# One decoder layer, prompt and samples: window copies spread over the projection, the second sample's chunks loaded early, the samples' sums a step earlier

## The chip, the cores and the metric

One NeuronCore of a Trainium2 chip runs the whole kernel in one launch. The metric is device time in microseconds (us). TensorE (PE) multiplies; VectorE (DVE), ScalarE (ACT) and GpSimd (POOL) compute elementwise; SyncE (SP) computes nothing and issues most of the DMAs; ACT issues the others. All arithmetic is float32; products that need the precision are made from a high part rounded to fp32r and the low remainder.

## The reference

One layer (D_MODEL 1024) for 512 prompt tokens and for 8 samples of one token each, the samples with 2048 cached positions in 16 pages of 128. Cut to what matters:

```python
z = rmsnorm(x) @ w_in                      # 1024 -> 2840 columns
q_sb, k_sb, v_sb, q_n, kv_c, kv_s, kv_w, gates = split(z)
# stick-breaking heads
s = q_sb @ k_sb.T / 8
log_1m = where(mask, log_sigmoid(-s), 0)
after = cumsum(log_1m, reverse=True) - log_1m
o_sb = where(mask, exp(log_sigmoid(s) + after), 0) @ v_sb
# NSA heads: compressed keys of chunks of 16, chosen blocks of 64, a window of 512
kc, vc = mlp(chunks of cached kv_c)        # silu(x @ w1) @ w2 on 32 positions
o_n = g0 * attend(kc, vc) + g1 * attend(top 16 blocks) + g2 * attend(window)
x = x + concat(rmsnorm(o_sb), rmsnorm(o_n)) @ w_out
x = x + square(relu(rmsnorm(x) @ w_up)) @ w_down
y = rmsnorm(x)
```

The new keys and values are outputs too, among them each sample's window buffer shifted by one row (`win_s`, 511 old rows of 1 KB copied).

## The kernel before

The engines run their own programs and meet through counting semaphores; the order on each engine is the order written in its program. The stages that the change touches follow each other:

**Projection.** `w_in` is worked through in 10 blocks of 284 columns (`NCB`, `CB`). Two buffers `win[u]` take the raw blocks; ACT rounds them (`win_high`, line 1261), DVE takes the remainder (`win_low`, line 1671), and PE makes 24 matmuls (8 slices of depth, 3 products) for each of four token tiles (`z_rows`). Between tiles 1 and 2 of block n stand 16 narrow matmuls for the 8 samples with the raw block n+1 (`z_samples`), so PE waits there for the load of block n+1. SP issues that load when DVE's one-element `memset` (line 1697) says that tile 3 of block n-1 is done. In the first block (`begin`) the remainder of slices 0 to 3 is made by POOL (line 2258), that of slices 4 to 7 by DVE (line 1660), and DVE also makes the low part of the activations (`gained_low`, line 1637). Ahead of the loop over the blocks ACT waits for the constants and issues the eight window copies (line 1284), HBM to HBM, 511 KB each.

**Samples' keys.** For each of 8 samples SP loads in `load_keys` 16 chunk DMAs of 128 KB for the *next* sample's compression (`load_chunks`, line 499, into `nat`, two homes in turn), 16 pages of selection keys (line 542, buffers `kquad`), 16 pages of stick-breaking keys (line 545, buffers `kring`) and the window (line 548). POOL reorders chunks (`permute`), PE transposes and multiplies (`compress`) and between the parts transposes the keys (`keys_T`), DVE scores the stick-breaking keys. Chunks of sample 0 come during the projection. `nat[1]` first serves the prompt's own compression (`nat_in10`), so sample 1's chunks are loaded only in `load_keys(0, 0, True)`.

**Attention.** 48 steps, written out for each engine: 16 of stick breaking, then 32 of NSA. The samples' small steps stand between them: `sample_sums` on PE at step 3 (8 wide float32 matmuls), `sample_logs` on DVE, an exponential on ACT at step 4, the accumulator's `memset` at step 4. The samples' values are spread by `value_steps` over the steps: page pairs (8 matmuls of 128x256 each) from step 5 on, 3, 3, 2 a sample for the first four samples, then one or two a step.

Of the kernel before, what the change touches and what calls it, by code (L numbers as in the profile page):

```python
# [21 lines left out]
ds = bass.ds  # L22

P = 128
# [3 lines left out]
B = 8  # L28
# [32 lines left out]
def value_steps():  # L61

    pairs, quads = [()] * (STEPS + 2), [()] * (STEPS + 2)
    at = 5
    for b in range(B):
        m = 0
        for n in ((3, 3, 2) if b < 4 else (2, 1, 1, 1, 1, 1, 1)):
            pairs[at] = tuple((b, m + j) for j in range(n))
            m, at = m + n, at + 1
    at = SB_U + 1  # L70
    for b in range(B):
        q = 0
# [44 lines left out]
def shape_constants():  # L117
# [3 lines left out]
    def put(name, a):  # L121
# [41 lines left out]
    "start_act": ["rt"] * 5 + ["w_hi_first", "gates_e"],  # L163
    "samples_pe": ["c_sc", "g_mm", "m_T", "c_scT", "m_b", "c_pT", "s_c", "c_imp", "c_selT", "c_mask", "m_den", "m_T", "m_b", "m_den", "v_ss"],
    "samples_dve": ["s_abs", "m_max", "c_s", "c_kbd", "m_diag", "s_sp", "c_nm", "m_sub", "s_suf", "c_p", "m_sum", "c_pg", "s_d", "acc_set", "c_sel",
                    "c_selx", "c_selm", "m_max", "m_rec", "m_diag", "m_sub", "m_sum", "m_rec", "w_set", "v_sq", "v_st", "v_cols"],
# [52 lines left out]
def decoder_step(nc, A, O):  # L219
    with ExitStack() as ctx:  # L220
# [115 lines left out]
        xT = [view(hT_at + i * 2048, KD, KVH, P) for i in range(2)]  # L336
        nat_at[1] = r.take(4096)
        nat = [[view(nat_at[u] + 2048 * half, CH // 2, 2, KVH, DH) for half in range(2)] for u in range(2)]
        hid = [view(r.take(256), KVH, P) for _ in range(4)]
        qb = view(r.take(2 * 512), 2, 512)  # L340
        kqT = view(x_at + 4228, 4, P)

# [127 lines left out]
        def _(sp):  # L470
# [39 lines left out]
            for u in range(2):  # L510
                load_block(u, FIRST // 2, u * CB)
                load_chunks(page_ids(8 * u), 0, u)
            load_columns(FIRST // 2 + 1, (NCB - FIRST) // 2 - 1, 2 * CB)

            sp.wait_ge(sem("rope_done"), T5)
# [3 lines left out]
            for t in range(T5):  # L519
                sp.wait_ge(sem(f"z_ev{t}"), NCB + 1)  # L520
            sp.wait_ge(sem("cmp_stored"), 16)
            sp.dma_start(nat[1][0][0:2 * (NCP + 1)].rearrange("p t k h d -> p (t k h d)"),
                O["cmp_p"][0, 0].rearrange("(c t) k h d -> c (t k h d)", t=CH // 2)).then_inc(sem("nat_in10"), 16)
            sp.dma_start(O["sb_p"][0, 0].rearrange("(t p) k h d -> p t (k h d)", p=P), z[:, 0:NT, O_KS:O_KS + 1024]).then_inc(sem("sb_stored"), 16)
# [29 lines left out]

            with sp.Fori(0, 3) as i:
                for u in range(2):
                    load_keys(i, u, True)
# [101 lines left out]
        def _(pe):  # L659
# [34 lines left out]
            def z_rows(i, u, t, begin=False):  # L694

                pe.wait_ge(sem(f"z_ev{t}"), i * 2 + u + 1)
                for k in range(KD):
                    if begin:
                        pe.wait_ge(sem("hT_ev"), k + 1)
                        if k == 0:  # L700
                            pe.wait_ge(sem("z_zero"), 2)
                        if k == KD // 2:
                            pe.wait_ge(sem("w_lo0"), 1 + 1)
                    for n, (h_, w_) in enumerate(((hT_r, win_hi_r), (hT_r, win_r), (hT_lo1_r, win_hi_r))):
                        ins = mm(bank[t][:, 0:CB], h_[:, k, t * P:(t + 1) * P], w_[u][:, k, :], k == 0 and n == 0, k == KD - 1 and n == 2)
                ins.then_inc(sem("z_mm"), 1)
# [414 lines left out]
            for s in range(STEPS + 2):  # L1121
# [16 lines left out]
                if 1 <= s < SB_U + 1:  # L1138
                    sb_sum(s - 1)
                if s == 3:  # L1140
                    sample_sums()
# [87 lines left out]
        def _(act):  # L1229
# [52 lines left out]
            wb, wo = A["state_nsa_win_kv"][0], O["win_s"][0]  # L1282
            for b in range(B):
                act.dma_start(wo[b, 0:WIN - 1].rearrange("(o s) k h d -> o (s k h d)", o=1),  # L1284
                    wb[b, 1:WIN].rearrange("(o s) k h d -> o (s k h d)", o=1)).then_inc(sem("kv_out"), 16)
            for turn, turns, col in COLUMNS:
                more = turn + turns < NCB // 2
                with act.Fori(0, turns if more else turns - 1) as i:
                    win_high(1, i + turn)
                    z_out(0, i, turn, col)  # L1290
                    win_high(0, i + turn + 1)
                    z_out(1, i, turn, col)
                if not more:
# [197 lines left out]
            for s in range(STEPS + 2):  # L1491
                if s in (5, 7, 9, 11):
                    cp_exp((s - 5) // 2)
                if s < SB_U:
                    sb_ln(s)
                if s == 4:
                    act.wait_ge(*signal("s_d", 1))
# [120 lines left out]
        def _(dve):  # L1618
# [35 lines left out]
            for t in range(2, NT):  # L1654
                row_scale(t, t + 2)
            for k in range(KD):
                gained_low(k)
                if k == 2:
                    dve.wait_ge(sem("w_hi0"), 1)
                    V.tensor_tensor(win_r[0][:, KD // 2:], win[0][:, KD // 2:], win_hi[0][:, KD // 2:], ALU.subtract).then_inc(sem("w_lo0"), 1)  # L1660
            dve.wait_ge(sem("z_zero"), 1)
# [309 lines left out]
            def small_steps(s):  # L1971
# [11 lines left out]
                if s == 3:  # L1983
                    cmp_groups()
                if s == 4:
                    dve.wait_ge(*signal("s_d", 1))
                    V.memset(bank[7][:, :], 0.0).then_inc(sem("samples_dve"), 1)
                    rank_greater()
                if s in (5, 7, 9, 11):
# [15 lines left out]
            def small_steps_late(s):  # L2005
# [3 lines left out]
                if s == 1:  # L2009
                    later_pages()  # L2010
                if s == 3:
                    sample_logs()
# [239 lines left out]
        def _(pool):  # L2252
# [4 lines left out]
            pool.wait_ge(*signal("w_hi_first", 1))  # L2257
            G_.tensor_tensor(win_r[0][:, 0:KD // 2], win[0][:, 0:KD // 2], win_hi[0][:, 0:KD // 2], ALU.subtract).then_inc(sem("z_zero"), 1)  # L2258

            pool.wait_ge(sem("qkT_mm"), 15)  # L2260

            def permute(c, kv, half, n):

                for hh in range(KVH):
                    ins = G_.tensor_copy(per(kv, hh, half)[0:n], nat[c % 2][half][0:n, :, kv, hh, :])
                ins.then_inc(sem("perm"), 1)

            pool.wait_ge(sem("nat_in10"), 16)
            for kv in range(2):
                permute(1, kv, 0, 2 * (NCP + 1))  # L2270
            for c in range(B):
                for kv in range(2):
                    for half in range(2):
                        if kv == 0:
                            pool.wait_ge(sem(f"nat_in{c % 2}{half}"), (c // 2 + 1) * 128 + (16 if c % 2 and half == 0 else 0))
                        if c == 0 and half == 1:
# [3 lines left out]
                        elif c:  # L2280
                            pool.wait_ge(sem("xT_mm1"), 4 * (c - 1) + 2 * kv + 2)
                        permute(c, kv, half, P)
            for n in range(1, KD):
# [38 lines left out]
```

## Time and profile before

| | |
|---|---|
| median of 3 runs | 1145.65 us (1145.42 to 1149.24) |
| the profiled execution | 1144.81 us, its span 1143.0 us |
| PE busy | 1061.2 us (93%) |
| DVE, ACT, POOL busy | 619.5, 391.3, 63.3 us |
| DMA | 177.59 MB, mean 155 GB/s |
| chain of waits, by engine | PE 61%, SP's queue 18%, issue 7%, DVE 5%, DMA 5%, ACT 3% |

The first row is what is compared; the second is the execution from which all durations come. The chain of waits follows the work that ended last back to what released it, so its shares say which engine set the end. An engine's busy share is an average over stages with different limits.

### The profile page before, as it was taken

What the parts mean: (1) busy time and instruction counts of PE and PEld (TensorE: products, weight loads), DVE (VectorE), ACT (ScalarE), POOL (GpSimd) and SP (SyncE); (2) the same over time, 40 slices, a digit from 0 to 9 for tenths busy, and PEclk for the clock granted to TensorE, in tenths of its full rate; (3) what the DMA queues carried; (4) which work ended last, traced back from release to release, by engine and by line L of the source; (5) the groups of instructions that cost most, each with busy time, mean ns of one, the idle gap of its engine ahead of it and who ended that gap; (6) DMA issues with size and microseconds to landing.
All of it is one profiled execution on the core that took longest, in us unless ns stands there. A gap on an engine that the chain in (4) does not pass through costs nothing.

```text
span 1143.0 us, 22964 instructions
## 1 busy us (share of the span) xinstructions
PE 1061.2 (93%) x8284; PEld 933.5 (82%) x8284; DVE 619.5 (54%) x1056; ACT 391.3 (34%) x729; POOL 63.3 (6%) x83
## 2 busy tenths in 40 slices
PE   6899998988989998899999889999999999998995
PEld 5899997887878886555555558999999999998995
DVE  5334664777768776775455445445533335553334
ACT  4111122333333335656454354322221112222124
POOL 1000003111111100000000000100000000000000
PEclk8899996989989895999998999999999999999998
DMA  8427539999999853356666762223333332333221
GB/s 295 151 89 201 129 98 227 250 248 258 269 261 260 246 182 120 121 175 226 204 208 194 214 203 75 75 74 92 110 92 91 92 83 84 91 92 93 90 78 75
DMA packets 180323, 177.59 MB, mean 155 GB/s; under 512 B 13128, under 2 KB 140869, under 8 KB 177893
## 3 DMA queue, kind: packets, MB, share of 16 engines
q1 hardware_dynamic: 178536, 169.72, 52.5%
q10 hardware_dynamic: 1724, 7.04, 1.8%
q8 instruction: 39, 0.64, 0.2%
q14 instruction: 24, 0.19, 0.1%
HBM read 170.83 MB, written 10.06 MB: 158 GB/s over the span
## 4 chain that ended last, share of the span: by engine, by line
PE 61%; SPq 18%; issue 7%; DVE 5%; DMA 5%; ACT 3%; ACTq 1%; POOL 0%; DVEq 0%; POOLq 0%
PE bank L664 59%; SPq L578 4%; SPq L499 3%; SPq L542 3%; SPq L545 3%; PE bank L668 3%; SPq L492 2%; DMA high_arena<-in_w_in_dram 2%; SPq L566 2%; DMA low_arena<-in_cache_nsa_slc_kv_dram 1%; DMA low_arena<-in_consts_dram 1%; DMA high_arena<-out_cmp_p_dram 1%; ACTq L1284 1%; DVE high_arena L2231 0%; DMA high_arena<-in_cache_nsa_slc_kv_dram 0%
## 5 line engine op out<-in xcount | busy, mean ns | idle before, releaser
L664 PE MATMUL bank<-high_arena 128*128 128x254 f32 (+8 forms) x1864 | 242.0, 349 | 11.9 <-ACT high_arena L1321 6.1
L664 PEld LDWEIGHTS bank<-high_arena 128*128 128x128 f32 (+5 forms) x1864 | 186.9, 153 | 49.8 <-issue 9.2
L2163 DVE TENSOR_TENSOR w_low<-high_arena,w_high 128x1024 fp32r<-128x1024 f32 x72 | 90.1, 1252 | 81.0 <-ACT w_high L1484 71.0
L1484 ACT ACTIVATE w_high<-high_arena 128x1024 fp32r<-128x1024 f32 x72 | 76.4, 1061 | 144.7 <-PE bank L664 144.7
L668 PE MATMUL bank<-low_arena 128*128 128x128 f32 (+3 forms) x658 | 103.2, 298 | 16.4 <-DMA low_arena<-in_cache_nsa_slc_kv_dram 10.4
L664 PE MATMUL bank<-a_high,w_high 128*128 128x256 f32 (+1 forms) x512 | 103.7, 284 | 5.3 <-issue 2.9
L668 PEld LDWEIGHTS bank<-low_arena 128*128 128x128 f32 (+3 forms) x658 | 83.0, 157 | 28.9 <-issue 12.3
L664 PE MATMUL bank<-h_high,w_high 128*128 128x256 f32 (+1 forms) x512 | 103.0, 282 | 1.8 <-DVE h_low L2187 1.8
L664 PE MATMUL bank<-a_low,w_high 128*128 128x256 f32 (+1 forms) x512 | 103.2, 283 | 0.0
L664 PE MATMUL bank<-h_low,w_high 128*128 128x256 f32 (+1 forms) x512 | 103.2, 283 | 0.0
L664 PE MATMUL bank<-h_high,w_low 128*128 128x256 f32 (+1 forms) x512 | 103.1, 283 | 0.0
L664 PE MATMUL bank<-a_high,w_low 128*128 128x256 f32 (+1 forms) x512 | 102.9, 282 | 0.0
L664 PE MATMUL bank<-w_in_high,h_high 128*128 128x284 f32 x320 | 97.3, 304 | 2.7 <-POOL w_in_low L2258 2.5
L1808 DVE TENSOR_REDUCE low_arena<-low_arena 128x512 f32 x128 | 87.9, 686 | 18.3 <-DVE low_arena L1804 0.6
L664 PE MATMUL bank<-w_in_low,h_high 128*128 128x284 f32 x320 | 95.8, 299 | 0.0
L664 PE MATMUL bank<-w_in_high,h_low_in 128*128 128x284 f32 x320 | 95.7, 299 | 0.0
L1804 DVE TENSOR_TENSOR low_arena<-low_arena,high_arena 128x512 f32<-128x512 f32 x120 | 86.8, 723 | 11.8 <-DMA low_arena<-in_cache_sb_kv_dram 11.7
L664 PEld LDWEIGHTS bank<-a_high,w_high 128*128 128x128 f32 x512 | 79.2, 188 | 6.1 <-issue 5.9
L664 PEld LDWEIGHTS bank<-h_high,w_high 128*128 128x128 f32 x512 | 79.3, 188 | 2.0 <-issue 2.0
L664 PEld LDWEIGHTS bank<-h_high,w_low 128*128 128x128 f32 x512 | 79.6, 188 | 0.0
L664 PEld LDWEIGHTS bank<-a_high,w_low 128*128 128x128 f32 x512 | 79.5, 188 | 0.0
L664 PEld LDWEIGHTS bank<-h_low,w_high 128*128 128x128 f32 x512 | 79.4, 188 | 0.0
(227 smaller groups left out, 1541.2 us busy)
## 6 DMA issues: line engine op xcount, KB each, us to landing
low_arena<-in_cache_sb_kv_dram SPq DMA_DIRECT2D x128, 256.0 KB, 4.8
high_arena<-in_cache_sb_kv_dram SPq DMA_DIRECT2D x128, 256.0 KB, 3.5
high_arena<-in_cache_nsa_cmp_kv_dram SPq DMA_DIRECT2D x128, 128.0 KB, 5.0
high_arena<-in_w_up_dram SPq DMA_DIRECT2D x32, 512.0 KB, 4.0
high_arena<-in_w_down_dram SPq DMA_DIRECT2D x32, 512.0 KB, 4.0
high_arena<-in_w_in_dram SPq DMA_DIRECT2D x10, 1136.0 KB, 5.9
low_arena<-in_cache_nsa_slc_kv_dram SPq DMA_DIRECT2D x128, 64.0 KB
high_arena<-in_cache_nsa_slc_kv_dram SPq DMA_DIRECT2D x128, 64.0 KB, 2.3
```

The lines of the kernel that those rows point to most:

```text
L492: return nc.values_load_multi_w_load_instructions(pt[0:1, ds(lo, 8)], engines=[mybir.EngineType.SP], min_val=0, max_val=NPHYS - 1, skip_ru ...
L499: sp.dma_start(nat[u][half][16 * p:16 * p + 16].rearrange("p t k h d -> p (t k h d)"), c_cmp[ds(pg, 1)].rearrange("o (c t) k h d -> (o c) ...
L542: sp.dma_start(kquad[n % 2][:, j], c_slc[ds(pages[p + j], 1), :, 0].rearrange("o s h d -> (o s) (h d)")).then_inc(sem(f"kq_in{n % 2}"), 16)
L545: sp.dma_start(kring[p], c_sb[ds(pages[p], 1), :, 0].rearrange("o s h d -> (o s) (h d)")).then_inc(sem(f"ring_in{p}"), 16)
L566: sp.dma_start(ring[:, u, :], c_sb[ds(pages[u], 1), :, 1].rearrange("o s h d -> (o s) (h d)")).then_inc(sem(f"ring_in{u}"), 16)
L578: sp.dma_start(quad[:, q, j, :], c_slc[ds(pages[4 * (q % 2) + j], 1), :, 1].rearrange("o s h d -> (o s) (h d)")).then_inc(sem(f"quad_in{q} ...
L664: return T.matmul(out, lhsT=l, rhs=r, start=start, stop=stop, **k)
L668: return T.transpose(out, in_, ident[0:n, 0:n])
L1484: S.activation(w_hi_r[u], w_raw[u], ACT.Copy).then_inc(sem(f"w_hi{u}"), 1)
L1804: chain(V.tensor_tensor(k, k, qb[:, u, :], ALU.mult))
L1808: V.tensor_reduce(raw_scores(ds(i, 1), u)[:, p, :], k.rearrange("p (h d) -> p h d", h=H), AX.X, ALU.add).then_inc(sem(f"ring_free{p % 8}"), 1)
L2163: V.tensor_tensor(w_lo_r[u], w_raw[u], w_hi[u], ALU.subtract).then_inc(sem(f"w_lo{u}"), 1)
```

## The change

1. `window_rows`: the window copies are issued inside ACT's loop over the blocks, one after each of blocks 0 to 7, instead of all ahead of it.
2. The first block's remainders: DVE makes slices 0 and 1 ahead of `gained_low`, POOL slices 2 to 7 in three pieces; PE waits for each piece at slices 0, 2, 4, 6.
3. `nat[1]` gets a home at the end of the memory, and the prompt's compression another (`nat_p`); sample 1's chunks are issued by SP after the last weight block, and `load_keys(0, 0, ...)` has none.
4. `sample_sums` and `sample_logs` move from step 3 to 2, ACT's exponential and the accumulator's `memset` from 4 to 3, the page pairs start at step 4, and sample 4's pairs go 3, 1, 1, 1, 0, 1, 0, 1.

```diff
-    at = 5
+    at = 4
-        for n in ((3, 3, 2) if b < 4 else (2, 1, 1, 1, 1, 1, 1)):
+        for n in ((3, 3, 2) if b < 4 else (3, 1, 1, 1, 0, 1, 0, 1) if b == 4 else (2, 1, 1, 1, 1, 1, 1)):
...
-        nat_at[1] = r.take(4096)
+        nat_at[1] = TOTAL - 304 - 4096
+        nat_p = view(kc_at, CH // 2, 2, KVH, DH)
...
             load_columns(FIRST // 2 + 1, (NCB - FIRST) // 2 - 1, 2 * CB)
+            sp.wait_ge(sem("z_mm"), 5 * NCB // 2)
+            for half in range(2):
+                load_chunks(page_ids(NPG + 8 * half), 1, half)
...
-            sp.dma_start(nat[1][0][0:2 * (NCP + 1)].rearrange("p t k h d -> p (t k h d)"),
-                O["cmp_p"][0, 0].rearrange("(c t) k h d -> c (t k h d)", t=CH // 2)).then_inc(sem("nat_in10"), 16)
+            sp.dma_start(nat_p[0:2 * (NCP + 1)].rearrange("p t k h d -> p (t k h d)"),
+                O["cmp_p"][0, 0].rearrange("(c t) k h d -> c (t k h d)", t=CH // 2)).then_inc(sem("nat_p_in"), 16)
...
-            with sp.Fori(0, 3) as i:
+            load_keys(0, 0, False)
+            load_keys(0, 1, True)
+            with sp.Fori(1, 3) as i:
...
                         if k == 0:
-                            pe.wait_ge(sem("z_zero"), 2)
-                        if k == KD // 2:
                             pe.wait_ge(sem("w_lo0"), 1 + 1)
+                        elif k % 2 == 0:
+                            pe.wait_ge(sem("z_zero"), k // 2 + 1)
...
-                if s == 3:
+                if s == 2:
                     sample_sums()
...
-            for b in range(B):
-                act.dma_start(wo[b, 0:WIN - 1].rearrange("(o s) k h d -> o (s k h d)", o=1),
-                    wb[b, 1:WIN].rearrange("(o s) k h d -> o (s k h d)", o=1)).then_inc(sem("kv_out"), 16)
+            def window_rows(b):
+
+                act.dma_start(wo[ds(b, 1), 0:WIN - 1].rearrange("o s k h d -> o (s k h d)"),
+                    wb[ds(b, 1), 1:WIN].rearrange("o s k h d -> o (s k h d)")).then_inc(sem("kv_out"), 16)
+
             for turn, turns, col in COLUMNS:
                 more = turn + turns < NCB // 2
                 with act.Fori(0, turns if more else turns - 1) as i:
                     win_high(1, i + turn)
                     z_out(0, i, turn, col)
+                    window_rows(i * 2 + 2 * turn)
                     win_high(0, i + turn + 1)
                     z_out(1, i, turn, col)
+                    window_rows(i * 2 + (2 * turn + 1))
...
-                if s == 4:
+                if s == 3:
                     act.wait_ge(*signal("s_d", 1))
                     f = sbs.rearrange("p b n j -> p (b n j)")
                     S.activation(f, f, ACT.Exp).then_inc(sem("samples_act"), 1)
...
+            dve.wait_ge(*signal("w_hi_first", 1))
+            V.tensor_tensor(win_r[0][:, 0:2], win[0][:, 0:2], win_hi[0][:, 0:2], ALU.subtract).then_inc(sem("w_lo0"), 1)
             for k in range(KD):
                 gained_low(k)
-                if k == 2:
-                    dve.wait_ge(sem("w_hi0"), 1)
-                    V.tensor_tensor(win_r[0][:, KD // 2:], win[0][:, KD // 2:], win_hi[0][:, KD // 2:], ALU.subtract).then_inc(sem("w_lo0"), 1)
...
                 if s == 3:
                     cmp_groups()
-                if s == 4:
                     dve.wait_ge(*signal("s_d", 1))
                     V.memset(bank[7][:, :], 0.0).then_inc(sem("samples_dve"), 1)
+                if s == 4:
                     rank_greater()
...
-                if s == 3:
+                if s == 2:
                     sample_logs()
...
-            G_.tensor_tensor(win_r[0][:, 0:KD // 2], win[0][:, 0:KD // 2], win_hi[0][:, 0:KD // 2], ALU.subtract).then_inc(sem("z_zero"), 1)
+            G_.tensor_tensor(win_r[0][:, 2:4], win[0][:, 2:4], win_hi[0][:, 2:4], ALU.subtract).then_inc(sem("z_zero"), 1)
+            pool.wait_ge(sem("w_hi0"), 1)
+            G_.tensor_tensor(win_r[0][:, 4:6], win[0][:, 4:6], win_hi[0][:, 4:6], ALU.subtract).then_inc(sem("z_zero"), 1)
+            G_.tensor_tensor(win_r[0][:, 6:8], win[0][:, 6:8], win_hi[0][:, 6:8], ALU.subtract).then_inc(sem("z_zero"), 1)
```

The lists of signals and POOL's waits follow these moves.

## Rows read from the trace of the kernel before

**Rows 1.** Windows: start:end, length, busy us (instructions) by engine, PE clock, DMA share, GB/s.
```profile
200.00:300.00 100.00, 92.60 (x557) 82.88 (x556) 74.03 (x117) 34.61 (x70) 17.66 (x26) 0.91 1.01 255
436.00:457.00 21.00, 18.34 (x62) 11.62 (x63) 13.39 (x41) 14.86 (x24) 0.00 (x0) 0.50 0.46 143
```
**Rows 2.** Chain of waits, 20 to 60 us: start, us, what.
```profile
14.76 8.83 DMA low_arena<-in_consts_dram
...
30.35 2.11 ACT w_in_high L1261
...
32.48 2.52 DVE w_in_low L1671
...
37.61 7.57 DMA high_arena<-in_w_in_dram
```
**Rows 3.** Timeline, 13 to 31 us: start, us, engine, line, operation, idle before.
```profile
14.64 2.60 POOL L2258 TENSOR_TENSOR w_in_low<-high_arena,w_in_high 128x1136 fp32r<-128x1136 f32 x1 [11.38 <-ACT w_in_high L1270]
...
17.39 0.57 PE L664 MATMUL bank<-w_in_high,h_high 128*128 128x284 f32 x1 [2.47 <-POOL w_in_low L2258]
...
18.03 1.33 DVE L1660 TENSOR_TENSOR w_in_low<-high_arena,w_in_high 128x1136 fp32r<-128x1136 f32 x1
...
23.62 6.44 ACTq L1284 DMA_DIRECT2D out_win_s_dram<-in_state_nsa_win_kv_dram  x8
```
**Rows 4.** Timeline, PE after its wait at 45 us: neighbours at either clock.
```profile
47.64 0.44 PE L664 MATMUL bank<-w_in_low,h_high 128*128 128x284 f32 x1
...
47.88 0.44 PE L664 MATMUL bank<-w_in_high,h_low_in 128*128 128x284 f32 x1
...
51.15 0.29 PE L664 MATMUL bank<-w_in_low,h_high 128*128 128x284 f32 x1
...
51.28 0.29 PE L664 MATMUL bank<-w_in_high,h_low_in 128*128 128x284 f32 x1
```
**Rows 5.** Timeline, where a block has landed (ACT) and PE's samples' matmuls start.
```profile
61.34 2.10 ACT L1261 ACTIVATE w_in_high<-high_arena 128x2272 fp32r<-128x2272 f32 x1 [5.28 <-DMA high_arena<-in_w_in_dram]
...
61.74 1.14 PE L664 MATMUL bank<-high_arena,low_arena 128*8 128x284 f32 x16
...
103.71 1.14 PE L664 MATMUL bank<-high_arena,low_arena 128*8 128x284 f32 x16 [0.37 <-DMA high_arena<-in_w_in_dram]
```
**Rows 6.** DMA queues, 24 to 38 us (packets, MB, share), then issues, 55.5 to 62 (KB, us).
```profile
q10 hardware_dynamic: 245, 4.19, 88.6%
...
high_arena<-in_w_in_dram SPq DMA_DIRECT2D x1, 1136.0 KB, 5.4
```
**Rows 7.** Samples' keys: timeline of SP and ACT, and the chain of waits.
```profile
194.34 4.19 SPq L499 DMA_DIRECT2D high_arena<-in_cache_nsa_cmp_kv_dram  x8
...
196.35 0.61 ACT high_arena L1334
...
210.64 0.46 SPq L548
...
300.99 0.45 SPq L548
...
222.95 0.28 ACT L1381 ACTIVATE high_arena<-bank 128x128 f32 x1 [1.26 <-PE bank L664]
249.76 0.28 ACT L1381 ACTIVATE high_arena<-bank 128x128 f32 x1 [1.45 <-PE bank L664]
```
**Rows 8.** Timeline, PE in the first attention steps.
```profile
450.04 2.08 PE L664 MATMUL bank<-low_arena 64*128 64x512 f32 x4 [0.69 <-ACT high_arena L1440]
...
457.16 3.71 PE L664 MATMUL bank<-high_arena,low_arena 128*128 128x512 f32 x8
...
460.80 0.49 PE L664 MATMUL bank<-low_arena 64*128 64x128 f32 x4
...
469.05 1.27 PE L664 MATMUL bank<-high_arena 128*8 128x256 f32 x20
...
499.50 0.62 PE L664 MATMUL bank<-high_arena 128*8 128x256 f32 x8 [1.07 <-DMA high_arena<-in_cache_sb_kv_dram]
```

More of the change, by code:

```diff
@@ L163 @@
     "start_act": ["rt"] * 5 + ["w_hi_first", "gates_e"],
-    "samples_pe": ["c_sc", "g_mm", "m_T", "c_scT", "m_b", "c_pT", "s_c", "c_imp", "c_selT", "c_mask", "m_den", "m_T", "m_b", "m_den", "v_ss"],
-    "samples_dve": ["s_abs", "m_max", "c_s", "c_kbd", "m_diag", "s_sp", "c_nm", "m_sub", "s_suf", "c_p", "m_sum", "c_pg", "s_d", "acc_set", "c_sel",
+    "samples_pe": ["c_sc", "g_mm", "m_T", "c_scT", "m_b", "s_c", "c_pT", "c_imp", "c_selT", "c_mask", "m_den", "m_T", "m_b", "m_den", "v_ss"],
+    "samples_dve": ["s_abs", "m_max", "c_s", "c_kbd", "m_diag", "s_sp", "c_nm", "m_sub", "s_suf", "c_p", "m_sum", "s_d", "c_pg", "acc_set", "c_sel",
                     "c_selx", "c_selm", "m_max", "m_rec", "m_diag", "m_sub", "m_sum", "m_rec", "w_set", "v_sq", "v_st", "v_cols"],
@@ L340, in decoder_step @@
         qb = view(r.take(2 * 512), 2, 512)
+        assert r.at <= nat_at[1]
         kqT = view(x_at + 4228, 4, P)
@@ L2257, in _, with permute @@
             pool.wait_ge(*signal("w_hi_first", 1))
-            G_.tensor_tensor(win_r[0][:, 0:KD // 2], win[0][:, 0:KD // 2], win_hi[0][:, 0:KD // 2], ALU.subtract).then_inc(sem("z_zero"), 1)
+            G_.tensor_tensor(win_r[0][:, 2:4], win[0][:, 2:4], win_hi[0][:, 2:4], ALU.subtract).then_inc(sem("z_zero"), 1)
+            pool.wait_ge(sem("w_hi0"), 1)
+            G_.tensor_tensor(win_r[0][:, 4:6], win[0][:, 4:6], win_hi[0][:, 4:6], ALU.subtract).then_inc(sem("z_zero"), 1)
+            G_.tensor_tensor(win_r[0][:, 6:8], win[0][:, 6:8], win_hi[0][:, 6:8], ALU.subtract).then_inc(sem("z_zero"), 1)
             pool.wait_ge(sem("qkT_mm"), 15)
-            def permute(c, kv, half, n):
+            def permute(src, kv, half, n):
                 for hh in range(KVH):
-                    ins = G_.tensor_copy(per(kv, hh, half)[0:n], nat[c % 2][half][0:n, :, kv, hh, :])
+                    ins = G_.tensor_copy(per(kv, hh, half)[0:n], src[0:n, :, kv, hh, :])
                 ins.then_inc(sem("perm"), 1)
-            pool.wait_ge(sem("nat_in10"), 16)
+            pool.wait_ge(sem("nat_p_in"), 16)
             for kv in range(2):
-                permute(1, kv, 0, 2 * (NCP + 1))
+                permute(nat_p, kv, 0, 2 * (NCP + 1))
             for c in range(B):
@@ L2274, in _ @@
                         if kv == 0:
-                            pool.wait_ge(sem(f"nat_in{c % 2}{half}"), (c // 2 + 1) * 128 + (16 if c % 2 and half == 0 else 0))
+                            pool.wait_ge(sem(f"nat_in{c % 2}{half}"), (c // 2 + 1) * 128)
                         if c == 0 and half == 1:
@@ L2281, in _ @@
                             pool.wait_ge(sem("xT_mm1"), 4 * (c - 1) + 2 * kv + 2)
-                        permute(c, kv, half, P)
+                        permute(nat[c % 2][half], kv, half, P)
             for n in range(1, KD):
```

## The prediction

> **What bounds the kernel now.** I read the busy shares first, then the windows by stage, then the chain of waits, then the timeline at the places the change touches. PE is busy 93% of the span and nearly all of the time behind 700 us, which the change leaves alone. In the samples' keys the DMA share is 1.01 while PE is busy 92.6 of 100 us [rows 1]: two resources end there almost together. In the projection PE is full, except at the start: the chain runs from the constants' DMA through ACT's issues of the window copies, ACT's rounding, DVE's remainder, and a weight load of 7.57 us [rows 2]. In the first attention steps PE runs at half clock [rows 1] and hands over to ACT and DVE and back. So a gain anywhere ahead of 700 us counts if it survives the next meeting of engines.
>
> **The change part by part.** All times are those of the profiled execution (span 1143.0, time 1144.81 us, 0.84 below the median of the runs).
>
> *First block's remainders.* PE starts at 17.39, released by POOL's 2.60 us for four slices [rows 3]. Now DVE makes two slices first: by its own 1.33 us for four [rows 3] some 0.67 us, from 14.6 (the end of ACT's rounding) to 15.3, then the first low part of the activations, 0.7, so PE starts at about 16.05: 1.3 us earlier. POOL's two-slice pieces take 1.3 each and are ready at 15.9, 18.1 and 19.4, while PE at half clock needs slice 2 at 17.5, 4 at 18.9, 6 at 20.3: no wait. DVE's 1.33 at 18.03, for which PE's later slices waited some 0.6, is gone from the middle. Ends of the gain: 1.2 (only the start), 2.5 (the wait too, and the clock rising sooner). I take 1.9.
>
> *Window copies: what the start gains.* The eight issues hold ACT 6.44 us from 23.62, ahead of the rounding of block 1 at 30.35; DVE's remainder follows at 32.48 and the release of `win[0]` behind it, so block 2's load leaves at 37.61, lands at 45.18 [rows 2, 3], and PE stands 3.0 us. Without the issues ACT rounds at 23.7, DVE is done at 30, and the load waits for PE's tile 3 alone: 35.9 before, 34.0 with the 1.9 above. A load takes 5.4 us with nothing beside it [rows 6], so 39.4, but the first copy is now issued beside it (below): 40.9. PE reaches that point at about 40.3 and so resumes at 41 instead of 45.23: 4.3 us. After the wait of 3.0 the granted clock was at its lower level: neighbouring matmuls stand 0.24 us apart (47.64, 47.88), later 0.13 (51.15, 51.28) [rows 4]. That was 16 matmuls of 0.11 too much, and the samples' 16 took 2.0 instead of 1.14 [rows 5]: 2.6 us, kept if a short stand leaves the clock alone. Together **-6.9** (with the 1.9 inside it).
>
> *Window copies: what the loop pays.* This is the term that decides. Tile 3's end releases both block n+2's load on SP and, through `z_out(t=3)`, the copy on ACT, within about half a us. PE needs that load 6.2 us later. The load landed at 61.34 and PE asked at 61.74; 0.4 us of slack there, and none at 103.71 [rows 5]; over the seven later blocks (61 to 145 us) I read 0 to 0.7, about 0.3. No row shows a copy beside a load. From above: the copies alone filled 88.6% of the 16 engines for 14 us, 12.4 us for eight, 1.55 each [rows 6]; if that time comes out of the load, it lands 1.5 later and PE stands 1.2. From below: if the copy waits behind the load or fits beside it, nothing. I take the upper end, because a load of 1136 KB in 5.4 us with its lead already fills the engines (share near 1 while its bytes flow), so there is no room beside it: seven more stands of 1.2, **+8.4**. The Trainium skill (DMA: Bandwidth & Descriptors, Queues, rings and completion order) says that each DMA engine takes turns between the queues for which it has work, a packet at a time; by it the copy's part on each engine is served in the middle of the load, the upper end. No row here shows it. Sample 1's 16 chunk DMAs stand behind load 9 as those of sample 0 behind load 6, which brought PE a wait of 0.37 [rows 5]: **+0.4**. Stands of this size also may lower the clock. Each lowering costs about 1.7 (the 16 x 0.11 of above); ends 0 and 8 of them. I take one: **+1.7**. Copies do not come late for anything: the last leaves some 40 us before the key stage.
>
> *Sample 1's chunks.* Gone from `load_keys(0, 0)`: 16 DMAs, 8.1 us of SP's issue (4.19 for eight [rows 7]), their four reads of page numbers, a wait for POOL, and 2 MB from the most crowded stretch. On the path this counts less. PE starts sample 0 at 196.35, released by ACT, and the chain returns to SP only at 210.64, where SP waits for PE to free a key buffer [rows 7]: whatever SP gains ahead of that it waits away. Behind it SP is never caught up again for some samples: 210.64 to 300.99 is three samples of 30.1, while PE alone needs 26.8 (249.76 - 222.95) [rows 7]. That 3.3 a sample is SP's issue and full DMA engines together. With 2 MB less queued at 210 the DMAs land sooner and SP's issues stall less. Ends: 0 (all lost at 210.64) and 8.1 (all kept). I take the excess of about one sample, **-3.5**. The chunks have their cover in the projection: the DMA engines idle there and SP's next work is at 161.8.
>
> *Samples' sums and values.* At step 3 the eight wide matmuls take 3.71 us at full clock, 457.16 to 460.87, and hold step 4's scores, which start at 460.80 [rows 8]; without them ACT would have released PE at 458.2, so 2.6 go. At step 2 they come at 449.4, where PE's spare is 0.69 [rows 8] and the clock is low (0.50 over 436 to 457 [rows 1]): up to 7.4 less 0.7, 6.7, for which the work behind, some already at full clock, gives back 1; net about +3 at step 4. The first three page pairs (24 matmuls, 1.5 us by 1.27 for 20 [rows 8]) now stand at step 4 ahead of step 5's scores and cost about 0.7 there. Against it: three pairs leave the steps behind 16, where PE is full, 1.5; and the wait of 1.07 for a value page at 499.50 [rows 8] goes, since the pages used there have been free for a step longer. Ends: +5 (low clock throughout, nothing back) and -3.5 (clock already up, or the wait hidden). I take **+1.3**.
>
> Sum: -6.9 + 8.4 + 0.4 + 1.7 - 3.5 + 1.3 = +1.4; 1144.8 + 1.4 = **1146.2 us**. Less than 0.5%, 5.7 us, either way is what a measurement of this kernel can't tell from no change.
>
> **The rivals.** *The copies don't hold the loads up.* For it: 6 to 9 us for a load would be much, the copies are only 4.2 MB, and they are issued some tenths behind. Against: the full share while a load's bytes flow. Then block 2's load lands at 39.4 and PE hardly waits: -8.3 instead of -6.9, no 8.4, no lowering; -8.3 + 0.4 - 3.5 + 1.3 = -10.1, 1134.7 us: faster. Chance 0.26.
>
> *Each stand costs the clock as well* (the slower side). Place: PE's samples' matmuls of blocks 1 to 8. Price: 1.7 each on top of the 1.2. It decides from about five of the eight on. For it: the samples' keys have lowered clock (0.91 over 100 us [rows 1]) with waits of only one to two us. Against: the 0.37 at 103.71 left it up, and PE is otherwise full here. All eight: 8.4 + 0.4 + 13.6 - 6.9 - 3.5 + 1.3 = +13.3, 1158.1; five: +8.2, 1153.0. Chance 0.20.
>
> *SP's freed time is kept whole* (-8.1 instead of -3.5): -3.2, 1141.6. For it: SP's issues run without a break from 210.64 for over 100 us. Against: the wait at 210.64 itself. Chance 0.16, most of it within 0.5%.
>
> **How the numbers follow.** Forecast 0.38, copies free 0.26, clock lost 0.20, SP's time kept 0.16. The forecast's own range is 1140 to 1152: within 0.5% in 0.28 of its 0.38, the rest evenly. With SP's 0.16 split 0.06 faster, 0.10 same; copies free 0.21 faster, 0.05 same; clock lost 0.16 slower, 0.04 same: faster 0.32, same 0.47, slower 0.21. The range 1134 to 1156 takes in the first rival and the second's nearer part, and leaves some 0.2 out.
>
> **What would show it.** PE's first product near 16.05; ACT's rounding of block 1 near 24; block 2's load issued near 34. A load in the loop taking about 6.9 instead of 5.4 us, and PE waiting 1 us or so for DMA in each of blocks 1 to 8: with 5.4 and no waits the first rival is right. The granted clock of 40 to 150 us: 1.00 but for one short dip, or falling block by block. The projection's end (ACT's last evacuation, 165.65) would be at about 169 by the forecast, 158 by the first rival. SP's window issue of sample 0 still directly behind PE, that of sample 3 within 87 instead of 90 us of it. The samples' sums at step 2 at some 7 us, and no wait at the first page of step 9. I am wrong if the projection ends earlier than before by several us, or if the key stage shrinks by more than 8.

## The result, and the profile after

| | median, us | runs |
|---|---|---|
| before | 1147.17 | 1145.42 to 1149.24 |
| after | 1170.25 | 1164.87 to 1177.55 |

The ratio is 1.0209, 95% interval 1.0166 to 1.0253: the changed kernel is about 24 us slower. All ratios here leave out the few executions that ran in the chip's slower state. The forecast was 1146.2 us, with a range up to 1156. The profiled execution of after took 1168.83 us, its span 1167.0 us.

I compared by stage first. In the changed kernel these windows (start:end, length, busy us and instructions of PE, weight loads, DVE, ACT, POOL, granted clock, DMA share, GB/s) answer to [rows 1]:

```profile
200.00:300.00 100.00, 89.10 (x532) 80.08 (x532) 71.23 (x114) 32.84 (x68) 18.47 (x26) 0.89 0.95 231
300.00:445.00 145.00, 126.44 (x733) 114.08 (x732) 100.86 (x162) 46.77 (x94) 20.85 (x30) 0.89 0.92 227
```

PE does less in the same time: 89.1 us of work in the 100 us from 200 on, 92.6 before. The milestones say where the 24 us arise. ACT's last evacuation of the projection, and ACT behind the first, third and last sample of the key stage, in after:

```profile
168.79 0.41 ACT L1273 ACTIVATE low_arena<-bank 128x284 f32<-128x284 f32 x1 [5.87 <-PE bank L671]
...
226.15 0.28 ACT L1392 ACTIVATE high_arena<-bank 128x128 f32 x1 [1.26 <-PE bank L671]
...
290.43 0.28 ACT L1392 ACTIVATE high_arena<-bank 128x128 f32 x1 [1.25 <-PE bank L671]
...
450.51 0.28 ACT L1392 ACTIVATE high_arena<-bank 128x128 f32 x1 [1.25 <-PE bank L671]
```

Before, the first of these was at 165.65 and the second at 222.95 [rows 7]; the last was here:

```profile
430.23 0.28 ACT L1381 ACTIVATE high_arena<-bank 128x128 f32 x1 [1.25 <-PE bank L664]
```

So 3.1 us are lost by the end of the projection, 17 more (20.3 in all) in the key stage, and the rest of the 24 behind it. The key stage's loss lies mostly in its second half: behind sample 3 (counted from 0) ACT stood at 312.39 us before and at 322.14 after, 6.6 us of the 17, and the other 10.5 us come in the four samples behind it.

```profile
312.39 0.28 ACT L1381 ACTIVATE high_arena<-bank 128x128 f32 x1 [1.25 <-PE bank L664]
```
```profile
322.14 0.28 ACT L1392 ACTIVATE high_arena<-bank 128x128 f32 x1 [1.25 <-PE bank L671]
```

In the key stage (215 to 445 us) these waits for DMA doubled. The first two rows are of after, the other two of before (columns: who, for what, us in all, times, longest):

```profile
DVE low_arena L1814 <- DMA low_arena<-in_cache_sb_kv_dram: 25.6, 11, 5.7
PE bank L675 <- DMA low_arena<-in_cache_nsa_slc_kv_dram: 24.1, 8, 6.8
```
```profile
DVE low_arena L1804 <- DMA low_arena<-in_cache_sb_kv_dram: 11.7, 9, 3.5
PE bank L668 <- DMA low_arena<-in_cache_nsa_slc_kv_dram: 10.4, 8, 2.4
```

These DMAs are issued by SP, and its timeline in after has a hole, answering to the 300.99 of [rows 7]:

```profile
309.12 0.44 SPq L553 DMA_DIRECT2D low_arena<-in_state_nsa_win_kv_dram  x1
315.61 0.36 SPq L536 DMA_DIRECT2D high_arena<-sb_queries  x1
```

Sample 3's last issue ends at 309.56, sample 4's first comes 6.05 us later, and the profile lists no wait of SP in between. It is where the two-turn loop `Fori(1, 3)` jumps back. The loop of the kernel before jumps back at the same place too, and there 0.64 us pass (300.99 + 0.45 to 302.08). Around the hole (309 to 318 us) an instruction queue moves three packets, and over the whole execution 30 where the page of before has 24:

```profile
q14 instruction: 3, 0.02, 0.9%
```
```profile
q14 instruction: 30, 0.25, 0.1%
```

The projection went nearly as forecast. In this order: the start in the timeline, the weight loads in the chain, TensorE's waits for them, and the window of the whole projection with its clock, 1.00 (answering to [rows 2 to 4]):

```profile
15.95 0.37 PE L671 MATMUL bank<-w_in_high,h_high 128*128 128x284 f32 x1 [0.91 <-DVE h_low_in L1648]
...
24.01 2.11 ACT L1268 ACTIVATE w_in_high<-high_arena 128x2272 fp32r<-128x2272 f32 x1 [3.86 <-DMA low_arena<-in_consts_dram]
```
```profile
34.31 8.27 DMA high_arena<-in_w_in_dram
...
50.53 6.62 DMA high_arena<-in_w_in_dram
```
```profile
PE bank L671 <- DMA high_arena<-in_w_in_dram: 10.8, 8, 2.3
```
```profile
0.00:166.00 166.00, 145.71 (x1142) 134.04 (x1143) 81.76 (x143) 39.79 (x52) 7.39 (x8) 1.00 0.55 164
```

### The profile page after: what moved, and what is told of

Same layout as the page of the kernel before. It is cut to its first block, busy times and chain, and to the rows that moved or that the text cites. A ratio compares the mean times of both kernels' runs of the same rounds, so it can differ in the third digit from the quotient of the medians.

```text
span 1167.0 us, 22958 instructions
## 1 busy us (share of the span) xinstructions
PE 1066.0 (91%) x8284; PEld 936.9 (80%) x8284; DVE 618.4 (53%) x1056; ACT 391.6 (34%) x729; POOL 65.8 (6%) x85
## 4 chain that ended last, share of the span: by engine, by line
PE 61%; SPq 14%; DMA 10%; issue 6%; DVE 4%; ACT 3%; ACTq 1%; POOL 0%; DVEq 0%; POOLq 0%
PE bank L671 57%; DMA high_arena<-in_w_in_dram 5%; PE bank L675 4%; SPq L585 3%; DMA low_arena<-in_cache_nsa_slc_kv_dram 3%; SPq L501 3%; SPq L547 2%; SPq L573 2%; SPq L494 2%; SPq L550 2%; DMA high_arena<-in_cache_sb_kv_dram 1%; DVE w_in_low L1681 1%; DMA high_arena<-out_cmp_p_dram 1%; ACT w_in_high L1268 1%; DVE high_arena L2241 0%
## 5 line engine op out<-in xcount | busy, mean ns | idle before, releaser
L671 PE MATMUL bank<-high_arena 128*128 128x254 f32 (+7 forms) x1864 | 243.0, 348 | 13.2 <-ACT high_arena L1332 6.1
L671 PEld LDWEIGHTS bank<-high_arena 128*128 128x128 f32 (+4 forms) x1864 | 187.7, 153 | 52.1 <-issue 13.2
L675 PEld LDWEIGHTS bank<-low_arena 128*128 128x128 f32 (+3 forms) x658 | 85.8, 161 | 43.4 <-DMA low_arena<-in_cache_nsa_slc_kv_dram 19.4
L671 PEld LDWEIGHTS bank<-a_low,w_high 128*128 128x128 f32 x512 | 79.4, 188 | 0.0
```

The source lines that it names most:

```text
L671: return T.matmul(out, lhsT=l, rhs=r, start=start, stop=stop, **k)
L675: return T.transpose(out, in_, ident[0:n, 0:n])
```

## The experiments

Each is timed beside the kernel before on the same chip. There the kernel before spread from 1138 to 1159 us over its runs, so the ratios with their intervals are what to read. Medians of before were 1146.8 to 1147.1.

### One part of the change at a time

**a: only the chunk part** (second home with its own place, sample 1's chunks behind the last weight block, samples 0 and 1 ahead of the key loop).

```
+            sp.wait_ge(sem("z_mm"), 5 * NCB // 2)
+            for half in range(2):
+                load_chunks(page_ids(NPG + 8 * half), 1, half)
...
-            with sp.Fori(0, 3) as i:
+            load_keys(0, 0, False)
+            load_keys(0, 1, True)
+            with sp.Fori(1, 3) as i:
```

> The kernel before with only the chunk part of the change: the second home has a place of its own, sample 1's chunks are loaded behind the last weight block, and the keys of sample 0 and 1 are issued without them or ahead of the loop. The changed kernel's key stage is 17 us longer (its sample ends come 20.3 us later at the end of the stage and 3.2 us later at its start), and its weight and chunk packets of 8192 bytes take 0.80 us in the mean instead of 0.66. Theory C (the chunk part makes that loss): 1162 to 1168 us, last sample of the key stage about 17 us later than before. Theory W (what the window copies beside the weight loads set up carries on): no loss here, 1142 to 1147 us, as the forecast had -3.5 and +0.4 for this part. Theory S (the samples' sums): also no loss here.

Measured: 1161.25 us, ratio 1.0094 (1.0056 to 1.0132). That is just below the range of theory C (from 1162) and far from the others. The key stage is 14 us longer, the projection unchanged, and the hole again, with nothing waited for:

```profile
302.58 0.45 SPq L553 DMA_DIRECT2D low_arena<-in_state_nsa_win_kv_dram  x1
308.00 0.36 SPq L536 DMA_DIRECT2D high_arena<-sb_queries  x1
```

**b: only the new places**, all loads in the old order (`nat_at[1] = TOTAL - 304 - 4096`, `nat_p`).

> The kernel before with only the places changed: second home at the top of memory, four half buffers and the query buffer 4096 elements lower, the page's leftover stripe loaded into a buffer of its own. All loads are issued in the old order. Theory H (the address at which the home lies, or its neighbours, costs DMA rate): 1155 us or more, with chunk packets near 0.80 us. Theory T (the early load and the order of issue it leaves behind do): 1146 to 1148 us, as before.

Measured: 1145.33 us, 0.9997 (0.9962 to 1.0032). The places cost nothing; theory H falls.

**c: only the window copies** moved into the loop over the blocks.

```
                     win_high(1, i + turn)
                     z_out(0, i, turn, col)
+                    window_rows(i * 2 + 2 * turn)
```

> The kernel before with only the sixteen window copies moved from the front of ScalarE's queue into the loop over weight blocks. The prediction had +8.4 for the stands of TensorE and -6.2 for the second block's earlier load: by it the last evacuation of the projection comes 0 to 4 us later and the kernel takes 1146 to 1151 us. Theory W (the copies are what slows the key stage): 1160 us or more, with the key stage some 17 us longer. Theory C: key stage within 2 us of before.

(There are eight copies, not the sixteen that this text says.) Measured: 1157.41 us, 1.0061 (1.0033 to 1.009), that is +7 us, more than the prediction's terms gave (1146 to 1151) and less than theory W. TensorE waits 10.1 us for weights in the projection instead of 3.4, and from the first to the last sample the key stage takes 209.2 us, 207.3 before. So the copies are a second loss, of their own.

**d: only the samples' sums and values** a step earlier (`if s == 2: sample_sums()` and the rest of that part).

> The kernel before with only the samples' sums, their exponent and the value steps one attention step earlier. The prediction had +1.3. The changed kernel gains another 6 us of delay within the first sixteen steps of attention. Theory S6 (this part makes those 6): 1151 to 1154 us, key stage as before. Theory L (they come from DMAs, value loads that are late for another reason): 1145 to 1149 us.

Measured: 1146.47 us, 0.9991 (0.9945 to 1.0036). Nothing: theory S6 falls.

**e: only the first block's remainders.**

> The kernel before with only the first block's remainders split over VectorE and GpSimd. The prediction had -1.9 us for it; the waits of TensorE for GpSimd's and VectorE's remainders in the first block were 2.5 us and below. By it 1144 to 1146 us, and the first product at about 16.05 instead of 17.39 us. Rival: TensorE waits for the later remainders instead, and the block ends where it did (1146 to 1148 us).

Measured: 1146.08 us, 0.9999 (0.9959 to 1.0039). The forecast's -1.9 lies inside the interval and can't be told from nothing.

### The loop on SP

**f: only the two samples written ahead of the loop.** Nothing else is changed, no load moves.

```
-            with sp.Fori(0, 3) as i:
+            load_keys(0, 0, True)
+            load_keys(0, 1, True)
+            with sp.Fori(1, 3) as i:
```

> The kernel before with one edit: the key loads of samples 0 and 1 stand ahead of the loop, which then runs twice instead of three times. Same loads, same order, same places; only SyncE's code is longer (six copies of the key loads instead of four). Theory F (SyncE is paced by its own issue, and the longer code makes it fetch instructions at the loop's end: with the chunk part alone, SyncE stands 4.97 us after the window issue at 302.58, with three packets of 8192 bytes on an instruction queue at 303.8, 306.4 and 308.8 us, none there before): 1153 to 1162 us, with such a hole of 4 to 6 us at the end of sample 3's loads and key stage 8 to 14 us longer. Theory E (the early load shifts the order in which DMA and TensorE free each other): 1145 to 1149 us and no hole.

Measured: 1162.56 us, 1.0146 (1.0068 to 1.0224). The key stage ends 17.2 us later, as in after, by an edit that moves no load. The hole, and the instruction queue in 302 to 310 us:

```profile
302.40 0.45 SPq L548 DMA_DIRECT2D low_arena<-in_state_nsa_win_kv_dram  x1
309.11 0.36 SPq L531 DMA_DIRECT2D high_arena<-sb_queries  x1
```
```profile
q14 instruction: 3, 0.02, 0.9%
```

**g: the chunk part with the loop turned**, so that SP has four copies of the key loads as before, not six.

```
             load_keys(0, 0, False)
-            load_keys(0, 1, True)
-            with sp.Fori(1, 3) as i:
-                for u in range(2):
-                    load_keys(i, u, True)
-            load_keys(3, 0, True)
+            with sp.Fori(0, 3) as i:
+                load_keys(i, 1, True)
+                load_keys(i + 1, 0, True)
```

> The chunk part of the change alone, as in the run with 1161.25 us, but with the loop turned: sample 0's keys ahead of it, three turns of (sample 2i+1, sample 2i+2) in it, sample 7's keys behind it, so that SyncE has four copies of the key loads as before. Theory F: the hole is gone and the time is 1143 to 1149 us. Theory E: still 1157 us or more.

Measured: 1148.98 us, 1.0014 (0.998 to 1.0048). The loss is gone with the early load still there, and so is the hole. This loop jumps back behind samples 2 and 4; 0.74 us (below) and 0.69 us pass there, as at the jumps of the kernel before, and no instruction packet moves at either:

```profile
272.30 0.45 SPq L553 DMA_DIRECT2D low_arena<-in_state_nsa_win_kv_dram  x1
273.49 0.36 SPq L536 DMA_DIRECT2D high_arena<-sb_queries  x1
```

What the window from 300 to 400 us looks like with the hole (f, first), in the kernel before with the same requests (second), and in g (third): PE busy 85.6, 92.5 and 94.3 us, and DMA with a share near 1 in all three, yet 239, 257 and 267 GB/s.

```profile
300.00:400.00 100.00, 85.56 (x492) 76.46 (x492) 66.96 (x107) 31.24 (x63) 16.27 (x24) 0.88 1.02 239
```
```profile
300.00:400.00 100.00, 92.45 (x552) 83.48 (x550) 76.02 (x120) 33.86 (x68) 19.67 (x28) 0.91 1.01 257
```
```profile
300.00:400.00 100.00, 94.25 (x560) 85.12 (x560) 76.22 (x121) 35.08 (x71) 19.80 (x30) 0.91 1.05 267
```

**h: the whole change with the turned loop.**

> The whole changed kernel with the turned loop. Theory F: what is left is the window copies' part (alone +6 to +10) less the first block's part: 1150 to 1159 us. Theory E: 1165 us or more, as the changed kernel (1170.25).

Measured: 1155.52 us, 1.0103 (1.0044 to 1.0161), 14.7 us below the changed kernel's median.

**k: all eight samples written out** in the kernel before, no loop; and **n: the last turn written out behind a two-turn loop**, which leaves the loop where it was.

> The kernel before with the key loads of all eight samples written out one after the other, no loop. Two more copies of that code than with the two-turn loop (1162.56). Theory F1 (what costs is the jump back to code that is no longer there): code read straight on is fetched ahead, no hole of 4 to 6 us at the end of sample 3's loads, 1145 to 1151 us. Theory F2 (any further code costs SyncE a fetch that it stands for): more holes, 1160 us or more.

> The kernel before with the last turn of the key loop written out behind it: two turns, then four copies, so as much code as with samples 0 and 1 ahead of the loop (1162.56), but the loop lies where it lay in the kernel before, directly behind SyncE's work for the projection. Theory P (what lies ahead of the loop decides whether its start is still there at the jump): no hole, 1144 to 1150 us. Theory N (the total amount of SyncE's code, or a loop of two turns, decides): a hole at the end of sample 1's loads (near 272 us), 1155 us or more.

Measured: k 1148.22 us, 1.0009 (0.9972 to 1.0045); n 1146.87 us, 1.0006 (0.9973 to 1.004). Neither more code (k, eight copies) nor a loop of two turns (n, six copies, as f) costs anything that shows: theories F1 and P. In n the jump back lies behind sample 1, at 240 us, and 0.68 us pass, as at the jumps of the kernel before:

```profile
239.94 0.45 SPq L548 DMA_DIRECT2D low_arena<-in_state_nsa_win_kv_dram  x1
241.07 0.35 SPq L531 DMA_DIRECT2D high_arena<-sb_queries  x1
```

What costs is a jump back with two copies of `load_keys` directly ahead of the loop (a, f, after, s); with one ahead (g, h, j, p) or none (before, b to e, n) there is no hole. The four with the hole share one thing more: their loop counts from 1, every other loop from 0. No run separates that, or where exactly the loop comes to lie in memory, from the two copies ahead.

### How 5 us become 15

**q, r: one stall of SP without a jump**, in the kernel with all loads written out: SP waits until its own last load has landed.

```
             for i in range(3):
                 for u in range(2):
                     load_keys(i, u, True)
+                if i == 1:                      # r: if i == 2, 960
+                    sp.wait_ge(sem("kq_in1"), 640)
```

> The kernel before with all key loads written out (1148.22), and with one stall of SyncE put in: after sample 3's loads it waits for its own last load, the window keys, to land (about 5 to 7 us, as the hole that the code fetch made). No code is fetched for it. The two-turn loop had a hole of 6.26 us there, and yet the key stage grew by 17.2 us (447.4 against 430.2). Theory A (SyncE's lead is gone, and from there on each key load is issued only when TensorE frees its buffer, so that its landing time shows in each sample behind): 1157 to 1166 us, the last three whole intervals between sample ends 31 us or more. Theory D (a stall costs its own length; the rest of the 17 us was the later fetches): 1151 to 1155 us.

> The same stall two samples later, after sample 5's loads. Theory A: fewer samples come behind it, 1152 to 1158 us. Theory D: 1151 to 1155 us, as after sample 3. So the difference of the two runs tells: 5 us or more by A, within 3 us by D.

Measured: q 1151.04 us, 1.0024 (0.9981 to 1.0068); r 1147.0 us, 1.0003 (0.9968 to 1.0038). The stall was 4.72 us long in q and cost 3 us or nothing. Theory A falls for a stall of this length; r lies below the range of theory D too, so SP catches up part of it. Both stalls were put into the kernel without a loop.

**t, u: more stall.** t adds a wait in sample 4 for its second half of chunks; u waits after sample 3 for the window keys and then also for the queries.

```
+                if c == 4:                      # u
+                    sp.wait_ge(sem("qb_in0"), 3 * 16)
```

> All key loads written out, with SyncE stalled at both places where the two-turn loop had a hole: after sample 3's loads (there 6.26 us, with one stall in this way 4.72), and in sample 4 behind its second half of chunks (there 4.42 us; here it waits for these chunks to land). One stall gave 1151.04, none 1148.22, the two-turn loop 1162.56. Theory T (the holes' time alone makes the loss, but only past a threshold, as the sum of both): 1157 to 1163 us, chunk packets from 300 us on at 0.85 us or more. Theory G (something else than SyncE's lost time goes with the jump back): 1150 to 1155 us, packets below 0.80.

> The same with one longer stall at one place: after sample 3's loads SyncE waits for the window keys, issues the queries of sample 4, and waits for these too, some 7 to 10 us in all. Theory T: 1156 us or more. Theory G: 1151 to 1156 us.

The second hole of 4.42 us that t was built on was misread: in f eight chunk issues run there, and 0.9 us behind them the next (row below, first); the hole doesn't exist. So t tells less than intended: its two stalls, 4.43 and 6.13 us, gave 1156.9 us, 1.0109 (1.0036 to 1.0182), 8.7 us above k, a little less than their own length. u gave 1157.91 us, 1.01 (1.0026 to 1.0175), 9.7 us above k for stalls of 4.60 and 3.66 us, 2.7 of the latter a wait (7.3 us lost in all):

```profile
324.85 3.84 SPq L499 DMA_DIRECT2D high_arena<-in_cache_nsa_cmp_kv_dram  x8
```
```profile
294.73 0.48 SPq L550 DMA_DIRECT2D low_arena<-in_state_nsa_win_kv_dram  x1
299.81 0.34 SPq L531 DMA_DIRECT2D high_arena<-sb_queries  x1
303.81 1.35 SPq L499 DMA_DIRECT2D high_arena<-in_cache_nsa_cmp_kv_dram  x3
```
```profile
300.00:400.00 100.00, 78.26 (x461) 70.12 (x460) 65.13 (x105) 30.17 (x61) 15.55 (x22) 0.87 1.02 238
```
```profile
low_arena<-in_cache_sb_kv_dram SPq DMA_DIRECT2D x48, 256.0 KB, 8.3
```

Here, with no jump back at all, the same slow transfers follow as in f and after: 238 GB/s at a share near 1 (k: 251 at 0.98), and the stick-breaking keys (last column, us from issue to landing) landing in 8.3 us, in after 7.4, before 5.0:

```profile
low_arena<-in_cache_sb_kv_dram SPq DMA_DIRECT2D x48, 256.0 KB, 7.4
```
```profile
low_arena<-in_cache_sb_kv_dram SPq DMA_DIRECT2D x53, 256.0 KB, 5.0
```

The table sets the runs side by side: where SP stood still, the time from ACT's end behind sample 3 to that behind sample 7, and how long a chunk's packet of 8192 bytes took in the mean (300 to 400 us).

| kernel | SP's stand, us | samples 4 to 7, us | packet, us |
|---|---|---|---|
| before, g, k, n | none | 117.8, 114.2, 118.4, 114.8 | 0.68, 0.76, 0.67, 0.64 |
| after, a, f, s | hole of 6.05, 4.97, 6.26, 5.41 | 128.4, 130.9, 132.0, 134.4 | 0.84, 0.82, 0.84, 0.84 |
| q | stall of 4.72 | 121.6 | 0.76 |
| t | stalls of 4.43 and 6.13 | 126.2 | 0.68 |
| u | stalls of 4.60 and 3.66 | 133.4 | 0.86 |

So u, without any jump, loses as much in these samples as the kernels with the hole, and its packets are as slow: theory T by both of its signs. t loses its time without slow packets, between the ranges of T and G. A stand of SP alone can thus set up the slow transfers, but q, with a stall nearly as long as the holes, did not.

### The window copies

**j: the whole change with the turned loop, copies behind ACT's rounding.**

```
                     win_high(1, i + turn)
+                    window_rows(i * 2 + 2 * turn)
                     z_out(0, i, turn, col)
-                    window_rows(i * 2 + 2 * turn)
```

> The whole changed kernel with the turned loop, and with each of the eight window copies issued right behind ScalarE's rounding of a weight block instead of right behind the evacuation that also releases the next weight load. The rounding ends some 6 us before the next load is issued (44.8 against 50.53 us), and a copy takes 1.5 to 3 us. Theory L (copy and load leave at the same moment and share the engines; that is the whole price of the copies): loads land in about 5.4 us again, TensorE's waits for weights fall from 10.6 to about 3 us, last evacuation of the projection near 162 us instead of 170.78, time 1143 to 1149 us, against 1155.52 without this edit. Rival (the copies cost by their bytes, wherever they lie in the projection): 1152 us or more.

**p: as h, without the eight copies.** **s: the changed kernel, two-turn loop, copies behind the rounding.**

> The whole changed kernel with the turned loop and without the eight window copies (that part of the output is left out, 7 MB of traffic). It gives the floor for the copies. Theory L: 1141 to 1147 us, no more than 3 us below the kernel with the copies behind the rounding; TensorE's waits for weights about 3 us. If the copies cost by their bytes, it is 6 us or more below it.

> The changed kernel, with its two-turn loop, and with the window copies issued behind ScalarE's rounding. It closes the square of the two causes: both mended 1143.19, copies alone still beside the loads 1155.52, neither mended 1170.25. If the two add up, 1156 to 1160 us (1170.25 less 12.3). If the two-turn loop costs less once the projection ends earlier (more room for SyncE ahead of sample 0), below 1153 us.

Measured: j 1143.19 us, 0.9971 (0.9937 to 1.0004); p 1143.63 us, 0.9967 (0.9934 to 1.0001); s 1155.36 us, 1.0064 (1.0028 to 1.01). With the copies in the gap between two loads they are as good as free (j and p agree; theory L). ACT's last evacuation starts at 160.21 us in j, 170.37 in h, and TensorE's waits for weights in the projection fall from 10.6 us (h, first) to 2.1 (j):

```profile
PE bank L669 <- DMA high_arena<-in_w_in_dram: 10.6, 8, 2.3
```
```profile
PE bank L669 <- DMA high_arena<-in_w_in_dram: 2.1, 3, 1.2
```

The four corners by medians: both as in the change 1170.25, loop mended 1155.52, copies mended 1155.36, both mended 1143.19. Loop 12.2 to 14.7, copies 12.3 to 14.9; by the ratios 11 to 12 and 15 to 17. Within that scatter the two add up. j beats the changed kernel by 27 us and has the best median of all; over the kernel before its gain of 0.3% isn't shown, the interval ends at 1.0004.

## Why the prediction was wrong

The step that failed is **sample 1's chunks**. It counted what leaves `load_keys(0, 0)` (8.1 us of issue, 2 MB) and took -3.5, ends 0 and -8.1. It measured +11 to +17 (by the ratios: a 10.8, f 16.7, after less h 12.2, s less j 10.7), and none of it comes from the chunks: it comes from the two calls written ahead of the loop, a cost that the term put at nothing. I had seen that SP issues without a break over that stretch, and still counted only the loads, not the code that issues them. None of the rivals held this. The early load itself gained nothing that shows either: in g (1.0014, 0.998 to 1.0048) the -3.5, a ratio of 0.997, lies outside the interval. The excess of 3.3 us a sample, on which it rested, was read against the shortest interval between two samples, 26.8 us; the seven of the kernel before run from 26.8 to 32.1, 29.6 in the mean.

**First block, start.** Product at 15.95 against 16.05 forecast, ACT's rounding at 24.01 (24), block 2's load issued at 34.31 (34). Right in place. The size of -1.9 could not be shown (e).

**What the start gains from the copies.** The load took 8.27 us, not 6.9, so it landed at 42.6 instead of 40.9. Part of the -6.9 was thus eaten at once. The clock was 1.00 over 0 to 166 us, 0.96 before, as the gain of 2.6 had it.

**What the loop pays.** The mechanism was right, and was the dearest part known in advance: from block 3 on the loads took 6.6, 6.6, 6.8, 7.4, 7.4, 6.9 and 8.4 us, before 5.4, 5.6, 5.4, 6.3, 6.1, 5.5 and 5.3. So beside a copy a load takes 1.0 to 1.4 us longer (forecast 1.5), and the last, with sample 1's chunks behind it as well, 3.1. TensorE waited 10.8 us in 8 blocks, 8.5 of it in the seven behind block 2 (forecast 8.4). The Trainium skill (DMA: Bandwidth & Descriptors, Queues, rings and completion order), by which an engine takes turns between queues, agrees with the trace: in after the copy's 16 data packets start when between a fifth and nine tenths of the load's 1024 have started, inside the load. And j shows that the cost is one of the moment, not of the bytes. No stand lowered the clock (1.00): the +1.7 was not paid, and the rival in which each stand costs the clock falls, as does that of free copies. The projection's end moved by +3.1 against +3.6 by the terms that come before it (-6.9 + 8.4 + 0.4 + 1.7). That these agree so well is partly luck: TensorE resumed in block 2 at 42.63 instead of 41, 1.6 us less gained, and the clock's 1.7, never paid, made up for it. c alone, without the first block's part, cost 7.

**Samples' sums.** 6.20 us at step 2 (forecast about 7, against 3.71 in [rows 8]):

```profile
469.41 6.20 PE L671 MATMUL bank<-high_arena,low_arena 128*128 128x512 f32 x8
...
493.86 0.62 PE L671 MATMUL bank<-high_arena 128*8 128x256 f32 x8 [1.19 <-DMA high_arena<-in_cache_sb_kv_dram]
```

The wait for a value page that stood in step 9 before (499.50 in [rows 8]) is gone, as forecast, but one of 1.19 us stands in step 5 instead (second row). In all the part is worth nothing that shows (d, 0.9945 to 1.0036; the forecast's +1.3 lies inside too). The 4 us that after loses behind the key stage have no cause shown: from ACT's last sample to the end it took 716.5 us, 712.8 before, and 714 to 723 in the other kernels that have the copies.

**The checks named.** From SP's window issue of sample 0 to that of sample 3 I forecast 87 us; it is 95.4 (213.70 to 309.12), 90.4 before. With 2 MB less queued the loads did not run ahead: h took 91.6 and g 92.2 over the same stretch. These rows refute the gain of 3.5. They end before the hole begins, so they say nothing of the loss behind it, and the 5 us that after loses here have no cause shown (s, with the same code on SP, took 91.0).

**What stays open.** That SP stands in the hole for instructions is the reading of three facts: no wait listed, three packets on the instruction queue around it and none at the jumps of g and n, and the hole coming and going with code ahead of the loop. Packets alone cause no stand: k moves three between 236 and 300 us, and SP issues on. The records don't name the cause of the stand, nor why two copies ahead bring it. Nor is it shown why holes of 5 to 6 us cost 11 to 17: a stall of 4.7 us cost 3, one of 7.3 us cost 9.7 and left the same slow transfers, so lost time on SP can do it, but the sizes don't lie on one line. No stall was put into a kernel with the loop.

## What to carry to other kernels

When an engine issues without a break, count its code as well as its work: here two calls peeled off the front of a loop were not free, while a rotated loop, a turn written out behind it, or no loop at all cost nothing that shows. Before believing a cause, run the edit without its purpose (f moved no load and had the whole loss). Look for a loop's price at the places where that loop jumps. A side transfer belongs in the gap between two loads that something waits for, behind the consumer of the last one, not on the event that releases the next.

## What the runs showed of the hardware

At a jump back in SP's loop 5.0 to 6.3 us passed without an issue where two copies of the key loads (50 DMA issues each; the first 34 in after, a and s) stood ahead of the loop, and 0.6 to 0.8 us with one or none; k, with the longest code and no jump, had no hole. The DMA engines, near a share of 1.0 either way, moved 257 GB/s from 300 to 400 us in the kernel before and 239 in f with the same requests, and 251 in k against 238 in u, which differ only in SP's stall. A 511 KB copy issued at the same moment as a 1136 KB load made the load land 1.0 to 1.4 us later (blocks 3 to 8: 6.6 to 7.4 us in after, 5.4 to 6.3 before); with the copies issued behind the rounding, as in j, the same loads took 5.2 to 6.5.
